# Decoder trunk step on eight cores: residual rows added by accumulating DMA, the mixing bias spread by matmuls, and three pieces of work moved

## The chip, the cores and the metric

The kernel runs on the 8 cores of one Trainium2 chip. Each core does one prompt sequence of 2048 positions and 64 sample rows (16 running sequences of 4 new tokens). No core talks to another. The metric is the device time in microseconds (us) of the slowest core.

## The reference

With x the residual rows, c the conditioning vector and D = 1024:

```python
mod = silu(c) @ w_ada + b_ada
shift, scale, gate = split(mod, 3)
h = rms_norm(x, g_norm) * (1 + scale) + shift
p = h @ w_in                                   # 3584 wide
h_a, b_a, c_a, z_a, u_b, v_b, z_b = split(p)
# group A: gated causal convolution of width 3
y_a = b_a * conv(c_a * h_a) * silu(z_a)
# group B: chunks of 128 positions, 8 heads
v_n = layer_norm(v_b)
y_b = u_b * (tril(w_s) @ v_n + b_s) * silu(z_b)
y = x + gate * (concat(y_a, y_b) @ w_out)
out = rms_norm(y, g_final)
```

Also returned are the last two rows of the convolution's input and the normalised v of the sample rows.

## The kernel before

Rows are worked in tiles of 128 positions and tiles in five blocks: 4, 4, 3 and the 64 sample rows, 3, and 2 tiles (`BLOCKS`, numbered 0 to 4). Channels lie on the partitions and positions along the free axis, so a projection is 8 matmuls of 128x128 weights against `hT` (up to 512 columns) into one PSUM bank. There are 8 banks, taken in turn by `nbank`, so a matmul group can start only when the engine that reads the group eight before it is done.

A block goes through two parts. In the **first part**, for j = 0 to 3, `A1` projects h and c (ACT copies the first out of its bank at L515, DVE multiplies at L523, ACT and DVE do the convolution at L534 and L541), and `A2` projects b and z (DVE L555, ACT L559, POOL L560 writes `yT`). After the pair of j = 2 (j = 1 in block 4) `V_group` projects v with the rows on the partitions (L601), DVE takes statistics (L616), and ACT writes the scaled `vn_bf` at L631. In the **gating part**, for j = 0 to 3, `GB` projects u and z (ACT L653, DVE L656), mixes `vn_bf` with `Wt` (PE L665), DVE adds the bias `bias2` (L675), and POOL multiplies into `yT` (L685). Between the steps of this part stands the **output step of the block before it**, one tile for each j: `C_mm` (PE L713, 16 matmuls of 512 columns), `C_s1` (DVE L729 and L730: times the gate, out of two banks; DVE L732: plus the residual rows, loaded again into `xc` by SP), `C_sq` (ACT L742: square sum), `C_s2` (DVE L800 and POOL L802: the power -1/2) and `C_s3` (DVE L811: times the norm factor, then a store by SP). `C_sq` of a tile is put off: `flush` issues it in the next `GB`, behind that `GB`'s first ACT instruction, and for the last tile of a block behind the gating part, which is ahead of the next block's first ACT copy (L515).

The input of the next block is made meanwhile: load into `xa`, square sum on ACT (`prep_sq`, L378), power on POOL (L380, L382), scaling on DVE (`prep_xn`, L389), transposes into `hT` (by PE for blocks 0 and 1, by DMA, L400, later), and `prep3`, the modulation with the adaLN scale and shift (ACT L428, DVE L432, for the sample columns DVE L443 and L446, which write all four k of a half).

Nothing reorders the work: every engine runs its instructions in the order in which the builder wrote them (`Sched`), and waits by semaphore at each. DMAs of the SP queue are issued by SP, the weights' and the first tiles' loads by POOL, in the same order of each queue's program. The bias `b_s` is brought to `bsT` by two SP loads that repeat one row over 64 partitions each (`late_loads_1`), and `bias2_ops` makes `bias2` of it.

Of the kernel before, what the change touches and what calls it, by code (L numbers as in the profile page):

```python
# [190 lines left out]
def build_nc(limit=None):  # L191
# [499 lines left out]
    def C_load(B, i, spare=None):  # L691
        ti, P, kind = B.tiles[i]
        R = slice(64, 128) if kind == "s" else slice(0, 128)
        src = x_s[0:64, :] if kind == "s" else x_p[(B.t0 + ti) * 128:(B.t0 + ti + 1) * 128, :]
        if spare is None:
            rc = nxt("xc", NXC)
            xt, xr = xc[rc], ("xc", rc)
        else:
            xt, xr = xa[spare], ("xa", spare)
        load("sp", xt[R, :], src, xr)  # L700
        cst[(B.i, i)] = [(xt, xr)]
# [474 lines left out]
```

How the kernel before makes its waits and increments, by code:

```python
        def run(e, eng):  # L113
            seen = {}
            nw = 0
            for o in streams[e]:
                need = {}
                waits = list(o.deps)
                if o.is_dma and o.prev is not None:
                    waits.append(o.prev)
                for d in waits:
                    key = d.sem.num
                    if key not in need or need[key][1] < d.val:
                        need[key] = (d.sem, d.val)
                for key, (sem, val) in need.items():
                    if seen.get(key, 0) >= val:
                        continue
                    eng.wait_ge(sem, val)
                    seen[key] = val
                    nw += 1
                ins = o.fn(eng)
                if o.is_dma:
                    ins.then_inc(o.sem, 16)
                elif o.needed:
                    ins.then_inc(o.sem, 1)
            stats[e] = (len(streams[e]), nw)
# [18 lines left out]
            @block.sync  # L155
            def _(eng):
                run("sp", eng)
                for q in self.QUEUES:
                    last = {}
                    for o in streams[q]:
                        if o.is_dma:
                            last[o.sem.num] = (o.sem, o.val)
                    for sem, val in last.values():
                        eng.wait_ge(sem, val)
```

## Time and profile before

| | us |
|---|---|
| median of 3 runs | 339.34 (338.82 to 340.24) |
| the profiled execution | 339.12 |
| its span, slowest core (4) | 337.3 |
| spans of the eight cores | 334.1 to 337.3 |
| busy: PE, DVE, ACT, POOL | 284.2, 187.7, 114.1, 110.7 |
| granted PE clock, mean | 0.968 |

1.8 us of the profiled execution lie outside the span. Times "at" a place count from the start of the span. On core 4, PE starts dense work at 48.9 us (block 0's second half of k), is in block 1 from 99.4 us, block 2 from 167.7, block 3 from 228.4, block 4 from 280.2, and ends its last matmul at 324.9. A busy PE means that matmuls are in flight, and idle time of PE before 325 us is what the path pays, as far as PE sets the end.

### The profile page before, as it was taken

How to read it: one execution, taken by the hardware profiler on the slowest of the kernel's cores; microseconds unless marked ns; L12 is line 12 of the kernel's file. 1: busy time of each engine (PE TensorE's matmuls, PEld its weight loads, DVE VectorE, ACT ScalarE, POOL GpSimd, SP SyncE). 2: the span in 40 equal slices, each digit the busy share in tenths (PEclk: the TensorE clock that was granted, in tenths of full speed). 3: DMA queues.
4: the chain of work that ended last, by engine and by line, in shares of the span. 5: the costliest groups of instructions: out<-in, count | busy, mean ns of one | idle time of the engine just before them, and what ended most of it. 6: DMA issues, size and time to landing. Idle time of an engine off the chain costs nothing.

```text
span 337.3 us, 5476 instructions; the slowest of 8 cores (334.1 to 337.3 us)
## 1 busy us (share of the span) xinstructions
PE 284.2 (84%) x1696; PEld 147.6 (44%) x1720; DVE 187.7 (56%) x350; ACT 114.1 (34%) x206; POOL 110.7 (33%) x161
## 2 busy tenths in 40 slices
PE   0325539999899999998989999999999999999840
PEld 0222214444454444443445454445555557766420
DVE  0321015445564454277887857658864666668982
ACT  2611013206552234311824245543216242232320
POOL 7294055214523531141224435121432112223210
PEclk9999858999999999999999999999999999999995
DMA  6999999999999992339327444212670102426223
GB/s 136 209 174 168 156 162 155 169 173 256 206 234 223 173 141 57 103 82 247 127 103 211 110 172 149 64 54 76 121 249 3 31 2 106 143 69 208 86 108 126
DMA packets 23148, 46.72 MB, mean 139 GB/s; under 512 B 10960, under 2 KB 11344, under 8 KB 22096
## 3 DMA queue, kind: packets, MB, share of 16 engines
q0 software_dynamic: 6624, 21.24, 35.0%
q1 hardware_dynamic: 16496, 25.14, 25.4%
q8 instruction: 14, 0.23, 0.3%
q14 instruction: 14, 0.11, 0.1%
HBM read 51.02 MB, written 8.85 MB: 178 GB/s over the span
## 4 chain that ended last, share of the span: by engine, by line
PE 42%; DMA 29%; DVE 12%; issue 7%; ACT 3%; POOL 3%; SPq 1%; DVEq 1%; POOLq 0%; ACTq 0%
PE pb L486 26%; DMA win_bf<-win_l 12%; DMA wada<-wada_l 11%; PE pb L713 8%; PE pb L601 4%; DVE ob L811 3%; DMA xa<-x_p 2%; DMA xc<-x_p 2%; DVE tmp L541 2%; DVE st L616 1%; PE pb L823 1%; ACT tmp L534 1%; POOL xa L314 1%; DVE ob L729 1%; DVE ob L730 1%
## 5 line engine op out<-in xcount | busy, mean ns | idle before, releaser
L486 PE MATMUL pb<-hT,win_bf 128*128 128x512 bf16 (+3 forms) x672 | 125.1, 341 | 2.0 <-DMA win_bf<-win_l 1.4
L486 PEld LDWEIGHTS pb<-hT,win_bf 128*128 128x128 bf16 x680 | 66.0, 98 | 57.5 <-issue 2.7
L713 PE MATMUL pb<-wout_bf,yT 128*128 128x512 bf16 (+1 forms) x246 | 56.6, 379 | 3.4 <-POOL yT L685 1.2
L486 PE MATMUL pb<-hT,wh 128*128 128x512 bf16 (+3 forms) x277 | 54.0, 356 | 4.7 <-ACT hT L428 3.6
L560 POOL TENSOR_TENSOR yT<-tmp,tmp 128x512 bf16<-128x512 f32 (+3 forms) x20 | 23.3, 1164 | 61.0 <-DVE tmp L555 32.3
L486 PEld LDWEIGHTS pb<-hT,wh 128*128 128x128 bf16 x280 | 27.8, 100 | 29.7 <-issue 9.8
L685 POOL TENSOR_TENSOR yT<-tmp,tmp 128x512 bf16<-128x512 f32 (+3 forms) x20 | 22.0, 1098 | 51.5 <-DVE tmp L675 27.6
L541 DVE SCALAR_TENSOR_TENSOR tmp<-spad,pv,tmp 128x512 f32<-128x512 f32 (+2 forms) x40 | 26.2, 656 | 20.7 <-ACT tmp L534 13.5
L713 PEld LDWEIGHTS pb<-wout_bf,yT 128*128 128x128 bf16 (+1 forms) x256 | 23.9, 98 | 29.9 <-issue 2.9
L601 PE MATMUL pb<-wv_bf,hT 128*128 128x512 bf16 (+1 forms) x133 | 29.6, 379 | 0.2
L742 ACT ACTIVATE junk<-ob 128x1024 bf16<-128x1024 f32 (+1 forms) x16 | 16.9, 1053 | 38.0 <-DVE ob L732 37.9
L389 DVE TENSOR_SCALAR xn<-xa,stat 128x1024 bf16<-128x1024 f32 (+1 forms) x17 | 13.7, 806 | 27.4 <-POOL stat L382 27.4
L428 ACT ACTIVATE hT<-hT,shT,aT 128x384 bf16<-128x384 bf16 (+2 forms) x28 | 18.0, 695 | 29.4 <-DVE aT L477 25.2
L534 ACT ACTIVATE tmp<-spad,pv 128x512 f32<-128x512 f32 (+2 forms) x20 | 12.7, 636 | 42.5 <-DVE spad L523 32.0
L523 DVE TENSOR_TENSOR spad<-pb,tmp 128x512 f32<-128x512 f32 (+2 forms) x20 | 11.7, 584 | 23.5 <-PE pb L486 11.6
L653 ACT ACTIVATE tmp<-pb 128x512 f32<-128x512 f32 (+3 forms) x20 | 10.3, 514 | 37.2 <-PE pb L486 37.2
L802 POOL TENSOR_TENSOR stat<-stat,mhalf 128x1 f32<-128x1 f32 x16 | 9.5, 596 | 37.2 <-DVE stat L800 24.5
L378 ACT ACTIVATE junk<-xa 128x1024 bf16<-128x1024 f32 (+1 forms) x17 | 17.9, 1054 | 11.1 <-DMA xa<-x_p 10.7
L732 DVE TENSOR_TENSOR ob<-ob,xc 128x1024 f32<-128x1024 f32 (+1 forms) x15 | 18.4, 1225 | 5.6 <-DMA xc<-x_p 3.3
L811 DVE SCALAR_TENSOR_TENSOR ob<-ob,stat,gf_bc 128x1024 f32<-128x1024 f32 (+1 forms) x16 | 20.5, 1279 | 1.5 <-POOL stat L802 1.4
L601 PEld LDWEIGHTS pb<-wv_bf,hT 128*128 128x128 bf16 (+1 forms) x136 | 13.3, 99 | 15.8 <-issue 0.4
L412 PE MATMUL pb<-ident,xn 128*128 128x128 bf16 x64 | 6.3, 263 | 16.0 <-DVE xn L389 16.0
(88 smaller groups left out, 252.9 us busy)
## 6 DMA issues: line engine op xcount, KB each, us to landing
y_p<-ob SPq DMA_DIRECT2D x15, 512.0 KB, 3.0
xc<-x_p SPq DMA_DIRECT2D x14, 512.0 KB, 6.9
wada<-wada_l POOLq DMA_DIRECT2D x6, 1024.0 KB, 35.4
xa<-x_p POOLq DMA_DIRECT2D x10, 512.0 KB, 39.1
win_bf<-win_l POOLq DMA_DIRECT2D x17, 256.0 KB, 42.7
xa<-x_p SPq DMA_DIRECT2D x8, 512.0 KB, 5.2
wout_bf<-wout_l POOLq DMA_DIRECT2D x2, 1024.0 KB, 57.7
wh<-winh_l POOLq DMA_DIRECT2D x4, 256.0 KB, 26.9
```

Of the source, the lines that this page charges most:

```text
L378: op("act", lambda e: e.activation(out=junk[0:P, :], in_=xa[ra][0:P, :], func=AF.Square, accum_out=ss), r=[("xa", ra)], w=[sres, "junk"])
L428: op("act", lambda e, k=k: e.activation(out=hb[:, k, 0:B.NP], in_=hb[:, k, 0:B.NP], func=AF.Identity, scale=aT[:, k, 0:1], bias=shT[:, k, ...
L486: ii = pe.matmul(bk.t[:, 0:B.N], lhsT=wsl(m, k), rhs=hT[B.h][:, k, 0:B.N], start=(k == 0), stop=(k == 7))
L534: ii = e.activation(out=c1[:, 0:NP], in_=spad[j][:, 2:2 + NP], func=AF.Copy, scale=cw(j, 2))
L541: ii = e.scalar_tensor_tensor(out=o[:, 0:NP], in0=spad[j][:, tp:tp + NP], scalar=cw(j, tp), in1=a[:, 0:NP], op0=ALU.mult, op1=ALU.add)
L560: op("pool", lambda e: e.tensor_tensor(out=yT[B.y][:, j, 0:N], in0=c2[:, 0:N], in1=sg[:, 0:N], op=ALU.mult), r=[c2r, sgr], w=[("yT", B.y, j)])
L601: ii = pe.matmul(bk.t[0:P, :], lhsT=hT[B.h][:, k, ti * 128:ti * 128 + P], rhs=wv_bf[:, k, :], start=(k == 0), stop=(k == 7))
L685: op("pool", lambda e: e.tensor_tensor(out=yT[B.y][:, 4 + j, 0:N], in0=tU[:, 0:N], in1=mb[:, 0:N], op=ALU.mult), r=[tUr, mbr], w=[("yT", B ...
L713: ii = pe.matmul(bk.t[R, :], lhsT=yT[B.y][:, k, ti * 128:ti * 128 + P], rhs=wout_bf[:, n, k, :], start=(k == 0), stop=(k == 7))
L732: op("dve", lambda e: e.tensor_tensor(out=o[R, :], in0=o[R, :], in1=xt[R, :], op=ALU.add), r=[ores, xr], w=[ores])
L742: op("act", lambda e: e.activation(out=junk[R, :], in_=o[R, :], func=AF.Square, accum_out=st[R, 0:1]), r=[ores], w=[sres, "junk"])
L811: op("dve", lambda e: e.scalar_tensor_tensor(out=o[R, :], in0=o[R, :], scalar=rs, in1=gf_bc[R, :], op0=ALU.mult, op1=ALU.mult), r=[ores, s ...
```

## The change

Five pieces. **One**: for the 15 output tiles of blocks 0 to 3, DVE's add of the residual rows (L732) and the SP loads into `xc` are gone. POOL issues, after DVE's two gate products, a DMA that reads the rows from `x_p` (or `x_s`) and adds them to `ob` in SBUF (`accum_op`). The square sum, the scaling and the store wait for this DMA. The two tiles of block 4 keep load and add. `ob` has 6 buffers for 3, in the room of `xc`. **Two**: the two repeating loads of `bsT` are replaced by a load of 2 rows, which DVE splits into three bf16 pieces (5 small instructions), and three matmuls with a 0/1 matrix (`sel`, three POOL instructions) that spread the sum of the pieces over the partitions; ACT copies the bank. This lies behind the first transposes. **Three**: in block 0, ACT scales v tiles 0 and 1 ahead of the convolution's first product of j = 3, and tiles 2 and 3 behind it, for all four behind it. **Four**: in block 1, `prep3` for block 2 moves from ahead of `GB` of j = 2 and 3 to behind `GB` of j = 1 and 2, ahead of the output step. **Five**: the multiply-add in `C_s2` (L800) moves from DVE to POOL, and in block 4 the final scaling of the last tile of block 3 moves from the step of j = 3 to behind `C_s1` of block 4's first tile.

```diff
-    NXC = 3
-    NOB = 3
+    NOB = 6
...
-    def A1(B, j):
+    def A1(B, j, mid=None):
...
+        if mid is not None:
+            mid()
         op("act", fc, r=sw + ["pv"], w=[c1r])
...
-        op("dve", lambda e: e.tensor_tensor(out=o[R, :], in0=o[R, :], in1=xt[R, :], op=ALU.add),
-           r=[ores, xr], w=[ores])
+        if own:
+            xt, xr = cst[(B.i, i)][0]
+            op("dve", lambda e: e.tensor_tensor(out=o[R, :], in0=o[R, :], in1=xt[R, :], op=ALU.add),
+               r=[ores, xr], w=[ores])
+        else:
+            src = x_s[0:64, :] if kind == "s" else x_p[(B.t0 + ti) * 128:(B.t0 + ti + 1) * 128, :]
+            op("pool", lambda e: e.dma_start(out=o[R, :], in_=src, accum_op=ALU.add), r=[ores], w=[ores], dma=True)
...
-        op("dve", lambda e: e.tensor_scalar(out=rs, in0=ss, scalar1=1.0 / D, scalar2=EPS, op0=ALU.mult, op1=ALU.add),
+        op("pool", lambda e: e.tensor_scalar(out=rs, in0=ss, scalar1=1.0 / D, scalar2=EPS, op0=ALU.mult, op1=ALU.add),
...
+    for q in range(3):
+        op("dve", lambda e, q=q: e.tensor_copy(out=bs_p[q], in_=bs_sb), r=["bias2"], w=[("vn", q)])
+        if q < 2:
+            op("dve", lambda e, q=q: e.tensor_tensor(out=bs_sb, in0=bs_sb, in1=bs_p[q], op=ALU.subtract),
+               r=["bias2", ("vn", q)], w=["bias2"])
+    bkb = nbank()
+
+    def fb(pe):
+        for q in range(3):
+            ii = pe.matmul(bkb.t[:, :], lhsT=sel, rhs=bs_p[q], start=(q == 0), stop=(q == 2))
+        return ii
...
-    def late_loads_1(g):
-        for half in range(2):
-            load("sp", bsT[64 * half:64 * half + 64, :, :].rearrange("p j t -> p (j t)"),
-                 bs_l[half].partition_broadcast(64), ("bsT", half), g)
...
-            A1(B, j)
+            A1(B, j, (lambda: V2(0, 2)) if b == 0 and j == 3 else None)
             if b == 0 and j == 3:
-                V2()
+                V2(2, 4)
...
-            if b == 1 and j >= 2:
-                prep3(NX, range(4 * j - 8, 4 * j - 4), "both")
...
+            if b == 1 and 1 <= j < 3:
+                prep3(NX, range(4 * j - 4, 4 * j), "both")
             if j < npv:
-                C_step(PV, j, (PV, j + NXC) if j + NXC < npv else None)
+                C_step(PV, j)
```

Where the instructions stand now. In the changed kernel the lines are numbered a few higher: L727 and L728 are the gate products (L729, L730 before), L736 the accumulating DMA, L745 the square sum (L742), L803 and L805 the norm factor (L800, L802), L429 and L433 to L447 the modulation (L428, L432 to L446), L661 and L680 the gating of `GB` (L656, L675), L516 the first copy of a block (L515).

On ACT, from the square sum of block 0's first output tile (`ob0`) to the first copy of block 2, before:

```order
L742 ACTIVATE junk_55,stat_82<-ob0_112 128x1024
L428 ACTIVATE hT0_47<-hT0_47,shT_76,aT_77 128x384 x2
L653 ACTIVATE tmp6_102<-pb4 128x512
L742 ACTIVATE junk_55,stat_82<-ob1_113 128x1024
L378 ACTIVATE junk_55,stat_82<-xa0_49 128x1024
L428 ACTIVATE hT0_47<-hT0_47,shT_76,aT_77 128x384 x2
L653 ACTIVATE tmp1_97<-pb1 128x512
L742 ACTIVATE junk_55,stat_82<-ob2_114 128x1024
L742 ACTIVATE junk_55,stat_82<-ob0_112 128x1024
L515 COPY tmp4_100<-pb5 128x448
```

and in the changed kernel:

```order
L745 ACTIVATE junk_55,stat_82<-ob0_109 128x1024
L429 ACTIVATE hT0_47<-hT0_47,shT_76,aT_77 128x384 x2
L658 ACTIVATE tmp6_102<-pb5 128x512
L745 ACTIVATE junk_55,stat_82<-ob1_110 128x1024
L429 ACTIVATE hT0_47<-hT0_47,shT_76,aT_77 128x384 x2
L379 ACTIVATE junk_55,stat_82<-xa0_49 128x1024
L658 ACTIVATE tmp1_97<-pb2 128x512
L745 ACTIVATE junk_55,stat_82<-ob2_111 128x1024
L745 ACTIVATE junk_55,stat_82<-ob3_112 128x1024
L516 COPY tmp4_100<-pb6 128x448
```

The second modulation stands ahead of the square sum of the next block but one's tile (`xa0`); each square sum of an `ob` now waits for a DMA.

On DVE, block 1's gating part, from the output product of tile 1 before:

```order
L729 TENSOR_TENSOR ob1_113<-pb1,gate_p_65 128x512
L730 TENSOR_TENSOR ob1_113<-pb2,gate_p_65 128x512
L732 TENSOR_TENSOR ob1_113<-ob1_113,xc1_110 128x1024
L800 TENSOR_SCALAR stat_82<-stat_82 128x1
L432 TENSOR_SCALAR hT0_47<-hT0_47,aT_77,shT_76 128x384 x2
L443 TENSOR_TENSOR tmp5_101<-hT0_47,aT_77 128x256
L446 TENSOR_TENSOR hT0_47<-tmp5_101,shT_76 128x4x64
L656 TENSOR_TENSOR tmp7_103<-pb3,tmp6_102 128x512
L675 SCALAR_TENSOR_TENSOR tmp8_104<-pb5,pv_78,bias2_68 128x512
L729 TENSOR_TENSOR ob2_114<-pb6,gate_p_65 128x512
L730 TENSOR_TENSOR ob2_114<-pb7,gate_p_65 128x512
```

and in the changed kernel, from `GB` of j = 1:

```order
L661 TENSOR_TENSOR tmp3_99<-pb7,tmp2_98 128x512
L680 SCALAR_TENSOR_TENSOR tmp4_100<-pb1,pv_78,bias2_68 128x512
L433 TENSOR_SCALAR hT0_47<-hT0_47,aT_77,shT_76 128x384 x2
L444 TENSOR_TENSOR tmp5_101<-hT0_47,aT_77 128x256
L447 TENSOR_TENSOR hT0_47<-tmp5_101,shT_76 128x4x64
L727 TENSOR_TENSOR ob1_110<-pb2,gate_p_65 128x512
L728 TENSOR_TENSOR ob1_110<-pb3,gate_p_65 128x512
L661 TENSOR_TENSOR tmp7_103<-pb4,tmp6_102 128x512
L680 SCALAR_TENSOR_TENSOR tmp8_104<-pb6,pv_78,bias2_68 128x512
L433 TENSOR_SCALAR hT0_47<-hT0_47,aT_77,shT_76 128x384 x2
L444 TENSOR_TENSOR tmp0_96<-hT0_47,aT_77 128x256
L447 TENSOR_TENSOR hT0_47<-tmp0_96,shT_76 128x4x64
```

The modulation of the first half (`hT0`) stands ahead of the product of tile 1, and that of the second half ahead of the product of tile 2 (which was ahead of it before); the add of 128x1024 is gone.

On POOL, block 4's gating part, from j = 0 before:

```order
L685 TENSOR_TENSOR yT0_95<-tmp6_102,tmp7_103 128x256
L685 TENSOR_TENSOR yT0_95<-tmp0_96,tmp1_97 128x256
L802 TENSOR_TENSOR stat_82<-stat_82,mhalf_83 128x1
L685 TENSOR_TENSOR yT0_95<-tmp3_99,tmp4_100 128x256
L802 TENSOR_TENSOR stat_82<-stat_82,mhalf_83 128x1
L685 TENSOR_TENSOR yT0_95<-tmp6_102,tmp7_103 128x256
L802 TENSOR_TENSOR stat_82<-stat_82,mhalf_83 128x1 x2
```

and in the changed kernel:

```order
L690 TENSOR_TENSOR yT0_95<-tmp6_102,tmp7_103 128x256
L736 DMA ob0_109<-x_p 128x1024
L690 TENSOR_TENSOR yT0_95<-tmp0_96,tmp1_97 128x256
L803 TENSOR_SCALAR stat_82<-stat_82 128x1
L805 TENSOR_TENSOR stat_82<-stat_82,mhalf_83 128x1
L736 DMA ob1_110<-x_p 128x1024
L690 TENSOR_TENSOR yT0_95<-tmp3_99,tmp4_100 128x256
L803 TENSOR_SCALAR stat_82<-stat_82 128x1
L805 TENSOR_TENSOR stat_82<-stat_82,mhalf_83 128x1
L736 DMA ob2_111<-x_p 128x1024
L690 TENSOR_TENSOR yT0_95<-tmp6_102,tmp7_103 128x256
```

Behind each `yT` product of j = 1 and 2 stands the norm factor of the tile before, and then the DMA of the tile of this step.

## Rows read from the trace of the kernel before

**Rows 1.** The page, busy time of each engine over the whole span.

```profile
PE 284.2 (84%) x1696; PEld 147.6 (44%) x1720; DVE 187.7 (56%) x350; ACT 114.1 (34%) x206; POOL 110.7 (33%) x161
```

**Rows 2.** The waits of PE: who waited for whom, us in total, times, longest.

```profile
PE pb L459 <- DMA wada<-wada_l: 14.0, 4, 4.9
...
PE pb L486 <- DMA win_bf<-win_l: 1.4, 1, 1.4
...
PE pb L486 <- DVE hT L446: 1.1, 1, 1.1
...
PE pb L713 <- DVE tmp L656: 0.9, 1, 0.9
```

**Rows 3.** The ten us from 80: busy by engine (count), clock, DMA share, GB/s.

```profile
80.00:90.00 10.00, 9.10 (x71) 4.50 (x69) 6.32 (x12) 6.44 (x12) 4.32 (x6) 1.00 1.05 224
```

**Rows 4.** Timeline of PE: start us, us, work, and idle before.

```profile
169.77 10.00 PE L486 MATMUL pb<-hT,wh 128*128 128x448 bf16 x52 [1.11 <-DVE hT L446]
...
194.29 9.26 PE L486 MATMUL pb<-hT,win_bf 128*128 128x448 bf16 x48
...
249.22 7.96 PE L486 MATMUL pb<-hT,win_bf 128*128 128x384 bf16 x48
...
320.86 0.59 PE L713 MATMUL pb<-wout_bf,yT 128*128 128x512 bf16 x2 [1.17 <-POOL yT L685]
```

**Rows 5.** The page, groups: the residual add on DVE, the power on POOL.

```profile
L732 DVE TENSOR_TENSOR ob<-ob,xc 128x1024 f32<-128x1024 f32 (+1 forms) x15 | 18.4, 1225 | 5.6 <-DMA xc<-x_p 3.3
...
L802 POOL TENSOR_TENSOR stat<-stat,mhalf 128x1 f32<-128x1 f32 x16 | 9.5, 596 | 37.2 <-DVE stat L800 24.5
```

**Rows 6.** The page, DMA issues: KB each, median us from issue to landing.

```profile
y_p<-ob SPq DMA_DIRECT2D x15, 512.0 KB, 3.0
...
xc<-x_p SPq DMA_DIRECT2D x14, 512.0 KB, 6.9
```

**Rows 7.** The DMA view, the 64 sample rows: KB, us to landing.

```profile
xc<-x_s SPq DMA_DIRECT2D x1, 256.0 KB, 3.5
```

**Rows 8.** The one load of `xa` issued at 177.8 us: its landing.

```profile
DMA to landing us min/median/max: 4.2/4.2/4.2
```

**Rows 9.** Timeline of DVE, gating part of block 1 and start of block 2.

```profile
152.28 0.68 DVE L730 TENSOR_TENSOR ob<-pb,gate_p 128x512 f32<-128x512 f32 x1
...
162.08 0.42 DVE L446 TENSOR_TENSOR hT<-tmp,shT 128x256 bf16<-128x256 f32 x1 [0.39 <-ACT hT L428]
...
169.54 0.75 DVE L389 TENSOR_SCALAR xn<-xa,stat 128x1024 bf16<-128x1024 f32 x1
...
172.06 0.68 DVE L730 TENSOR_TENSOR ob<-pb,gate_p 128x512 f32<-128x512 f32 x1
```

**Rows 10.** Timeline of ACT over the same stretch, and in block 2.

```profile
156.22 1.06 ACT L742 ACTIVATE junk<-ob 128x1024 bf16<-128x1024 f32 x1 [7.12 <-DVE ob L732]
...
160.67 1.31 ACT L428 ACTIVATE hT<-hT,shT,aT 128x384 bf16<-128x384 bf16 x2 [3.30 <-DMA hT<-xn]
...
175.34 0.51 ACT L515 COPY tmp<-pb 128x448 f32<-128x448 f32 x1
...
198.66 2.11 ACT L631 ACTIVATE vn_bf<-pb,stat 128x512 bf16<-128x512 f32 x3 [6.48 <-DVE stat L625]
```

**Rows 11.** Timeline of ACT in block 3 and at the start of block 4.

```profile
252.43 2.11 ACT L631 ACTIVATE vn_bf<-pb,stat 128x512 bf16<-128x512 f32 x3 [6.06 <-DVE spad L519]
...
284.81 0.37 ACT L515 COPY tmp<-pb 128x256 f32<-128x256 f32 x1
```

**Rows 12.** Timeline of DVE, last block.

```profile
281.41 0.69 DVE L730 TENSOR_TENSOR ob<-pb,gate_s 64x512 f32<-64x512 f32 x1
...
304.93 0.68 DVE L730 TENSOR_TENSOR ob<-pb,gate_p 128x512 f32<-128x512 f32 x1
...
325.05 0.68 DVE L768 TENSOR_TENSOR ob<-pb,gate_p 128x512 f32<-128x512 f32 x1
```

**Rows 13.** Timeline of POOL, last block.

```profile
319.99 0.72 POOL L685 TENSOR_TENSOR yT<-tmp,tmp 128x256 bf16<-128x256 f32 x1 [3.33 <-DVE stat L800]
```

More of the change, by code:

```diff
@@ L268, in build_nc @@
     vnS = A("vnS", [64, 512], F32)
+    sel = vn_bf[3][0:2, 0:128]
+    bs_sb = bias2[0:2, :, :].rearrange("p j t -> p (j t)")
+    bs_p = [vn_bf[q][0:2, :] for q in range(3)]
     yT0_off = (A.off + 63) // 64 * 64
@@ L276, in build_nc @@
     A.off = mark
-    NXC = 3
-    NOB = 3
-    xc = [A(f"xc{i}", [128, D], F32) for i in range(NXC)]
+    NOB = 6
     ob = [A(f"ob{i}", [128, D], F32) for i in range(NOB)]
@@ L585, in build_nc, with V2 @@
     vlate = []
-    def V2():
-        while vlate:
-            vlate.pop(0)()
+    def V2(q0=0, q1=4):
+        for f in vlate:
+            f(q0, q1)
+        if q1 == 4:
+            vlate.clear()
     def V_group(B, kind, grp, mid):
@@ L626, in V_group, with scale_v @@
                                                    op0=ALU.mult, op1=ALU.mult), r=[sres], w=[sres])
-        def scale_v():
-            for q, (ti, _) in enumerate(grp):
+        def scale_v(q0, q1):
+            for q, (ti, _) in list(enumerate(grp))[q0:q1]:
                 bk = bks[q]
@@ L689, in build_nc, with C_load @@
     cst = {}
[L691 to L701, printed above, removed]
+    def C_load(B, i):
+        load("sp", xa[i][:], x_p[(B.t0 + i) * 128:(B.t0 + i + 1) * 128, :], ("xa", i))
+        cst[(B.i, i)] = [(xa[i], ("xa", i))]
     def C_mm(B, i, k0, k1):
@@ L706, in C_mm @@
         if k0 == 0:
-            cst[(B.i, i)] += [nbank(), nbank()]
-        b0, b1 = cst[(B.i, i)][1:3]
+            cst[(B.i, i)] = cst.get((B.i, i), []) + [nbank(), nbank()]
+        b0, b1 = cst[(B.i, i)][-2:]
         def fn(pe):
@@ L720, in C_s1 @@
         R = slice(64, 128) if kind == "s" else slice(0, 128)
-        (xt, xr), b0, b1 = cst[(B.i, i)]
+        own = B.i == len(PB) - 1
+        b0, b1 = cst[(B.i, i)][-2:]
         g = gate_s if kind == "s" else gate_p
@@ L873, in build_nc @@
     cnt["xa"] = 0
+    load("sp", bs_sb, bs_l[:, :], "bias2")
     load("sp", st_sb[:].rearrange("p j s r -> p (j s r)"), stT[:, :], "st_sb")
@@ L881, in build_nc @@
        r=["ident"], w=["ident"])
+    op("pool", lambda e: e.memset(sel, 1.0), w=[("vn", 3)])
+    op("pool", lambda e: e.affine_select(out=sel, in_=sel, compare_op=ALU.is_ge, fill=0.0, base=0,
+                                         pattern=[[1, 128]], channel_multiplier=-64), r=[("vn", 3)], w=[("vn", 3)])
+    op("pool", lambda e: e.affine_select(out=sel, in_=sel, compare_op=ALU.is_ge, fill=0.0, base=63,
+                                         pattern=[[-1, 128]], channel_multiplier=64), r=[("vn", 3)], w=[("vn", 3)])
     for i, n in ((0, 2), (2, 2), (4, 3)):
@@ L891, in build_nc @@
     prep2(B0, 3, "act")
+    for q in range(3):
[8 more added lines that the diff above has]
+        return ii
+    op("pe", fb, r=[("vn", 3)] + [("vn", q) for q in range(3)], w=[bkb.res])
+    op("act", lambda e: e.copy(out=bsT[:].rearrange("p j t -> p (j t)"), in_=bkb.t[:, :]),
+       r=[bkb.res], w=[("bsT", 0), ("bsT", 1)])
     for i, n in ((0, 2), (2, 2), (4, 3)):
@@ L966, in C_step @@
         cq.append((B, i))
-        if nload is not None:
-            C_load(*nload)
         if len(cq) >= 3:
@@ L985, in build_nc @@
         late = b < 2
-        def first_c():
-            for i in range(min(NXC, npv)):
-                C_load(PV, i)
         if last:
             for i in range(len(B.tiles)):
-                C_load(B, i, i)
+                C_load(B, i)
         for j in range(4):
@@ L1108, in build_nc @@
             C_s1(B, 0)
+            C_s3(PV, npv - 1)
             C_mm_half(B, 1, 0)
```

11 lines of the change are left out of this document (2 added, 9 removed).

## The prediction

> **What bounds the kernel now.** I read four views in this order. The page gives PE 284.2 us of a span of 337.3 [rows 1], so PE carries the path but is idle for 53 us. The waits of PE say where: 14.0 us for the first weights, all before 48.9 us, and then little: 1.4 for a weight DMA late in block 0, 0.9 for DVE in block 1, 1.1 for the modulated input of block 2 [rows 2], 1.2 for the last `yT` [rows 4]. Behind PE's end at 324.9 us lie 12.4 us of closing work. So what can be won between 49 and 325 us is about 5 us, and much can be lost: PE runs dense only because the other engines hand back its 8 banks in time. The third view, the timelines of DVE and ACT, tells how much slack that has. The fourth, the DMA issues, tells how long a transfer takes to land.
>
> The DVE work taken away is large (the add takes 1.225 us [rows 5], 15 times), but its place is taken by a transfer on the same chain: gate product, residual, square sum on ACT. ACT is in order, so whatever stands behind the square sum waits for that DMA too. Call A the time from POOL's issue to the landing.
>
> **The price A.** No accumulating DMA is in the trace. Below stand the plain stores of the same 512 KB, 3.0 us, and above the loads into `xc`, 6.9 us in the median, which mostly ran three together [rows 6]. A single load of 512 KB from `x_p` took 4.2 us [rows 8]. The new DMA reads as much from `x_p` and also reads and rewrites `ob`, and POOL's issue is a little longer than SP's. The nearest row is the single load; I take A = 4.5, and keep 3.0 to 6.6. For the 64 sample rows the load took 3.5 [rows 7], 0.7 less than the full one, so A - 0.7 there.
>
> **Part by part.** A step from engine to engine is taken as 0.1 to 0.15 us: ACT ends its modulation at 160.67 + 1.31 = 161.98, DVE's L446 starts at 162.08 [rows 9, 10].
>
> *Startup.* Five small DVE instructions, three matmuls and three POOL instructions come at 5 to 24 us. PE waits there for weights anyway (14.0 us [rows 2]), and the first 48.9 us are bound by DMA: 0. If that cover were gone it would be about 1 us.
>
> *Bias load.* 256 KB of repeated rows leave the DMA engines in block 0, where these are saturated (share 1.05, 224 GB/s at 80 us [rows 3]): 256 KB at that rate is 1.2 us, by which the later weights land sooner. The wait there is 1.4: **-1.2**. The v tiles scaled sooner take some 0.6 us off PE's wait for banks before that, but the same weight DMA then sets the start: 0 (bounds of both together -2.0 and -0.5).
>
> *Block 1, gating.* The gate products of tile 0 end at 152.28 + 0.68 = 152.96 [rows 9], now 151.8. From there: steps, issue and landing 0.25 + A; square sum with its read 1.15; then ACT's half of the first modulation, 1.31 [rows 10], since it stands behind this square sum; DVE's L446, which waits for it (0.39 us already now [rows 9]), 0.5; only then the products of tile 1, 1.3. Then the same round again for tile 1 and the second half: 0.25 + A + 1.15 + 1.31 + 0.6. The input of block 2 is whole at 151.8 + 7.8 + 2A = 159.6 + 2A. Now it is at 169.77 [rows 4]; PE would be there at 168.66 - 0.87 - 1.2 = 166.6. With A = 4.5: 168.6. So **-1.2 against now** (this takes in the -1.2 above): the wait of 1.1 and that of 0.9 are not won but paid to the DMA. It is 2A - 10.2, never under -3.2.
>
> *Block 1 to 2.* Call E the time at which that input is whole. Behind E, DVE now has to do the products of tile 2 (1.3, before E until now), wait for POOL, which issues a DMA and runs two pairs for norm factors (a power 0.6 each [rows 5]) before the one that L389 needs (ends E + 4.7; it starts at 169.54 now [rows 9]), L656 and L675 (1.3), the products of tile 3 (1.3): E + 7.3, against 2.97 now (172.74 [rows 9]). Then DMA, square sum, and the first copy of block 2: it ends at E + 7.3 + 0.25 + A + 1.15 + 0.5 = E + 9.2 + A; now 175.34 + 0.51 [rows 10], E + 6.1. That is 3.1 + A later. What hangs on it is a chain of DVE and ACT, with no room in it, up to `vn_bf` in the same block: its first scaling ends at 199.4 [rows 10] and frees the bank in which PE puts u. PE's 48 matmuls from 194.29 are six groups of 1.54, u the fifth: it starts at 200.45 [rows 4]. Slack 1.05. So PE stands still for 3.1 + A - 1.05: **+6.5** with A = 4.5. Sum so far +5.3.
>
> *Block 2 to 3.* Here the order is the old one, and the add is replaced by the DMA: the first copy comes A - 1.7 later. The slack, read the same way, is 2.6 (the last of the three scalings from 252.43 [rows 11] against PE's mixing matmuls, after 249.22 and six groups [rows 4]): **+0.2**.
>
> *Block 3 to 4.* The products of the sample tile end at 282.1 [rows 12], the copy at 285.18 [rows 11]. They can start 0.4 sooner, since `ob` has six buffers. With A - 0.7 = 3.8 for the sample rows the copy comes 3.8 - 1.7 = **+2.1** later, and in block 4 (256 columns) the slack is only some 0.5, so DVE's chain and with it the end go by the whole.
>
> *Block 4 and the end.* Products of tile 0 end at 304.93 + 0.68 [rows 12] + D, where D is the shift so far. Its factor is ready A + 2.5 later; POOL issues the DMA of tile 1 behind it, so tile 1's factor comes at 310.6 + 2A + D; DVE's scaling of tile 1 (1.28) stands ahead of L656 and L675 (0.85) and POOL's last `yT` (0.8): 313.5 + 2A + D, which is 322.5 + D; now 319.99 + 0.72 = 320.7 [rows 13]: **+1.8**. Behind it DVE reaches L768 after 4.3 us now (325.05 [rows 12]); then it also waits for the factor of tile 2, A - 0.55 behind `yT`, and scales (1.28): A + 0.75 = 5.25: **+0.9**. The three adds gone here (3.7 us) are thus cover for waits, not a gain.
>
> Sum: -1.2 + 6.5 + 0.2 + 2.1 + 2.7 = +10.3. On the profiled execution's 339.1 that is **349.4 us**; the median of the runs is 339.34, 0.2 above it. All terms go by A: for A = 3.6 the sum is +4.2 (343.3), for A = 5.3 it is +16.7 (355.8), some 7 us for each us of A.
>
> **A rule against a row.** The row of plain stores says 3.0 us for 512 KB [rows 6], a load 4.2 [rows 8]. The Trainium skill (DMA: Bandwidth & Descriptors, Anatomy of one DMA, SWDGE path) gives for a DMA issued by GpSimd about 2.0 us plus the bytes over 436 GB/s, which is an estimate of 3.2 us here, and nothing extra for an accumulate; that would make the sum about +1.9, 341.0 us. No row shows this form of DMA.
>
> **The rivals.**
> (1) *The landing is as short as a store's.* A = 3.0: the input of block 2 is bound by PE (-3.2), 1.0 behind DVE's chain, so the stall in block 2 is 5.05 - 1.0; block 4's copy gives +1.3, the end -0.8. Sum +1.3: 340.4 us. For it: the stores. Against it: every load took longer.
> (2) *Faster.* The mechanism is that the square sums find their tile landed. It decides at A of about 2.8, by the sum above; with A = 2.0, as the 256 KB stores at the end take, the waits of 0.9 and 1.1 us and those of the end are won: -3.2, a stall of 4.05 - 3.0 in block 2, +0.3 into block 4, -1.7 at the end, sum -3.5: 335.6 us. For it: if my chain from the first copy of block 2 to `vn_bf` has more room than 1.0 us, the largest term falls away. Against it: the rows' 512 KB transfers.
> (3) *The landing is that of loads in company*, A over 5.3 up to 6.6, because the DMA moves each row twice or POOL writes its descriptors late. The sum is +17 to +27, middle 360 us. Against it: the DMA engines have room from 150 us on. The Trainium skill (SBUF — State Buffer, Who interferes with whom) says that DVE's two-port forms lock GpSimd out of the port with which it writes descriptors; that would lengthen A where L432 or L389 follows the product. No row here shows a DMA issue so held.
>
> **How the numbers follow.** My case (A 3.6 to 5.3) 0.58, rival 1 0.13, rival 2 0.16, rival 3 0.13. The range from 334.5 to 356.0 takes in all but rival 3 and a few strays. A measurement of this kernel tells about 0.5% from no change, 337.6 to 341.0: faster 0.16, same 0.13, slower 0.71.
>
> **What would show it.** In the changed profile: the accumulating DMA's landing, 4.5 us; ACT's square sum waiting for it, also ahead of the first copy of blocks 2, 3 and 4, with 6.4 us between the last gate product's end and that copy's end (3.1 now); PE idle some 6 us between 175 and 210 us, little at 260, some 2 us at 290 to 300; no wait for weights late in block 0; PE at block 2 near 168.6; POOL's last `yT` near 332. A landing under 3 us, or a dense PE in block 2, would refute the forecast.

## The result: 365.76 us, 7.6% slower

| | before | changed |
|---|---|---|
| median, us | 339.32 (338.82 to 340.24) | 365.76 (363.78 to 366.73) |
| ratio, 95% interval | | 1.0758 (1.0729 to 1.0788) |
| profiled execution; its span, slowest core | 339.12; 337.3 | 365.2; 363.6 |
| granted PE clock, that core | 0.968 | 0.949 |

The direction was forecast, the size was not: 349.4 us was said, with 356.0 as the upper end. Rival 3 (landings of 5.3 to 6.6 us, about 360 us) is the case that came, near its upper end. Medians below are over all executions of a kernel; the ratios leave out the few in which the cores of one die ran slower.

The page of the changed kernel, busy time of each engine and the DMA issues (KB, median us from issue to landing), to be read against [rows 1, 6]:

```profile
PE 298.1 (82%) x1723; PEld 149.3 (41%) x1723; DVE 171.8 (47%) x324; ACT 114.8 (32%) x207; POOL 129.8 (36%) x195
...
y_p<-ob SPq DMA_DIRECT2D x15, 512.0 KB, 4.8
ob<-x_p POOLq DMA_DIRECT2D x14, 512.0 KB, 6.2
```

DVE has 16 us less to do, as planned, and the span is 26.3 us longer. The median landing is 6.2 us, where the forecast took 4.5. PE's busy time grew too, by 13.9 us, and its idle time (span less busy) only from 53.1 to 65.5; what lies in the busy time is told in the last section.

The waits of ACT and of PE (us in total, times, longest), for [rows 2]:

```profile
ACT junk L745 <- DMA ob<-x_p: 86.3, 14, 12.2
...
PE pb L487 <- DVE ob L728: 4.5, 2, 4.2
PE pb L487 <- ACT tmp L516: 4.1, 2, 3.7
PE pb L710 <- POOL yT L690: 3.9, 1, 3.9
...
PE pb L487 <- DVE tmp L558: 2.4, 2, 1.8
PE pb L487 <- ACT vn_bf L636: 2.1, 2, 1.2
PE pb L487 <- DVE hT L447: 2.0, 1, 2.0
```

All 15 square sums of these tiles wait for their DMA: 14 in the row above, and that of the sample tile for 3.0 us. From block 1 on PE never waits for a DMA itself; it waits for DVE, ACT and POOL in turn, and the chain shows how these stand behind ACT. Here is the chain that ended last, over 150 to 200 us (start, us, what):

```profile
150.04 0.68 DVE ob L728
...
151.35 8.81 DMA ob<-x_p
...
161.45 1.21 ACT hT L429 x2
...
163.69 0.69 DVE ob L728
...
164.99 7.22 DMA ob<-x_p
...
174.00 0.70 ACT hT L429
...
182.14 1.10 POOL yT L690
...
183.73 7.30 DMA ob<-x_p
...
192.32 0.43 ACT tmp L516
```

Gate product, DMA, square sum, modulation, next gate product, DMA: this is the round that the forecast wrote down, twice in block 1 and once more into block 2, with 8.8, 7.2 and 7.3 us where it put 4.5. PE over the same stretch and at the end ([rows 4] before):

```profile
164.52 3.57 PE L487 MATMUL pb<-hT,win_bf 128*128 128x512 bf16 x8 [4.20 <-DVE ob L728]
...
175.37 0.92 PE L487 MATMUL pb<-hT,wh 128*128 128x448 bf16 x4 [2.04 <-DVE hT L447]
...
192.89 4.87 PE L487 MATMUL pb<-hT,win_bf 128*128 128x448 bf16 x16 [3.68 <-ACT tmp L516]
...
215.57 3.19 PE L487 MATMUL pb<-hT,win_bf 128*128 128x448 bf16 x16 [0.93 <-ACT vn_bf L636]
...
346.19 0.59 PE L710 MATMUL pb<-wout_bf,yT 128*128 128x512 bf16 x2 [3.90 <-POOL yT L690]
```

The input of block 2 is whole at 175.37 (169.77 before), block 3 starts at 243.65 (228.44), block 4 at 298.10 (280.20), and the last `yT` is done at 346.05 (320.7). These are the slowest cores of either profile, core 5 here and core 4 before.

### The profile page after: what moved, and what is told of

It reads as the page before. It is cut to its first block, busy times and chain, and to the rows that moved or that the text cites. A ratio compares the mean times of both kernels' runs of the same rounds, so it can differ in the third digit from the quotient of the medians.

```text
span 363.6 us, 5517 instructions; the slowest of 8 cores (357.6 to 363.6 us)
## 1 busy us (share of the span) xinstructions
PE 298.1 (82%) x1723; PEld 149.3 (41%) x1723; DVE 171.8 (47%) x324; ACT 114.8 (32%) x207; POOL 129.8 (36%) x195
## 4 chain that ended last, share of the span: by engine, by line
PE 34%; DMA 27%; DVE 13%; issue 12%; POOL 5%; ACT 4%; DVEq 1%; SPq 1%; POOLq 0%; ACTq 0%
PE pb L487 20%; DMA ob<-x_p 13%; DMA wada<-wada_l 10%; PE pb L710 8%; PE pb L606 5%; DVE tmp L544 2%; DVE st L621 2%; DMA xa<-x_s 2%; DMA ob<-x_s 1%; DVE spad L524 1%; DVE ob L728 1%; ACT tmp L535 1%; ACT junk L745 1%; DMA hT<-xn 1%; POOL yT L690 1%
## 5 line engine op out<-in xcount | busy, mean ns | idle before, releaser
L487 PE MATMUL pb<-hT,win_bf 128*128 128x512 bf16 (+3 forms) x680 | 130.6, 348 | 13.1 <-DVE ob L728 4.2
L487 PEld LDWEIGHTS pb<-hT,win_bf 128*128 128x128 bf16 x680 | 66.3, 99 | 73.2 <-issue 20.9
L710 PE MATMUL pb<-wout_bf,yT 128*128 128x512 bf16 (+1 forms) x256 | 58.5, 381 | 5.6 <-POOL yT L690 3.9
L487 PE MATMUL pb<-hT,wh 128*128 128x512 bf16 (+3 forms) x280 | 57.4, 367 | 5.4 <-DVE hT L433 2.9
L745 ACT ACTIVATE junk<-ob 128x1024 bf16<-128x1024 f32 (+1 forms) x16 | 16.9, 1058 | 89.5 <-DMA ob<-x_p 86.3
L487 PEld LDWEIGHTS pb<-hT,wh 128*128 128x128 bf16 x280 | 28.4, 103 | 33.2 <-issue 14.8
L544 DVE SCALAR_TENSOR_TENSOR tmp<-spad,pv,tmp 128x512 f32<-128x512 f32 (+2 forms) x40 | 27.0, 674 | 21.1 <-ACT tmp L535 14.7
L429 ACT ACTIVATE hT<-hT,shT,aT 128x384 bf16<-128x384 bf16 (+2 forms) x28 | 18.1, 698 | 21.8 <-DVE aT L478 20.5
L736 POOL DMA_DIRECT2D ob<-x_p x14 | 12.9, 922 | 31.6 <-DVE ob L728 15.8
L636 ACT ACTIVATE vn_bf<-pb,stat 128x512 bf16<-128x512 f32 x16 | 11.4, 778 | 27.2 <-DVE stat L630 16.4
L381 POOL TENSOR_SCALAR stat<-stat 128x1 f32<-128x1 f32 (+1 forms) x17 | 4.3, 250 | 38.9 <-ACT junk L379 38.0
```

What stands on the lines that cost most here:

```text
L429: op("act", lambda e, k=k: e.activation(out=hb[:, k, 0:B.NP], in_=hb[:, k, 0:B.NP], func=AF.Identity, scale=aT[:, k, 0:1], bias=shT[:, k, ...
L487: ii = pe.matmul(bk.t[:, 0:B.N], lhsT=wsl(m, k), rhs=hT[B.h][:, k, 0:B.N], start=(k == 0), stop=(k == 7))
L544: ii = e.scalar_tensor_tensor(out=o[:, 0:NP], in0=spad[j][:, tp:tp + NP], scalar=cw(j, tp), in1=a[:, 0:NP], op0=ALU.mult, op1=ALU.add)
L710: ii = pe.matmul(bk.t[R, :], lhsT=yT[B.y][:, k, ti * 128:ti * 128 + P], rhs=wout_bf[:, n, k, :], start=(k == 0), stop=(k == 7))
L745: op("act", lambda e: e.activation(out=junk[R, :], in_=o[R, :], func=AF.Square, accum_out=st[R, 0:1]), r=[ores], w=[sres, "junk"])
```

## Experiments

The kernels of one group ran on one chip, with runs of the kernel before beside them; ratios are to those. The edits are shown cut (`...`) and without the switches that select them in the kernels that ran.

### Is it the DMA, or the new order?

`e1_no_accum` undoes part one and keeps parts two to five.

```diff
-    NOB = 6
+    NXC = 3
+    NOB = 3
...
-            op("pool", lambda e: e.dma_start(out=o[R, :], in_=src, accum_op=ALU.add), r=[ores], w=[ores], dma=True)
+            op("dve", lambda e: e.tensor_tensor(out=o[R, :], in0=o[R, :], in1=xt[R, :], op=ALU.add),
+               r=[ores, xr], w=[ores])
```

> Part one of the change is undone: residual rows are loaded into `xc` by SP and added by DVE, with three buffers of each, as before; the parts two to five (bias by matmuls, v tiles, third block's modulation, norm factor on POOL) stay. My theory: all of the loss hangs on the accumulating DMA between gate product and square sum, and the other parts win the two small waits of block 1 and the weight wait. Then 336 to 340 us, input of block 2 whole at 168 to 169, block 2's stall gone. Rival: the new order by itself costs, since DVE's products of tiles 2 and 3 come behind the modulation and the norm factors move to POOL: then 345 us or more, with block 2's last gating groups still late on PE.

Measured 339.61 us beside 339.55, ratio 1.0006 (0.9983 to 1.0028). The rival falls: parts two to five cost nothing. Nor do they win anything that is measured. In the profiled execution, averaged over the eight cores, block 1's first matmul comes at 98.0 us for 99.2, as much as the forecast had for the bias load, and the mean span is 334.5 us for 335.6. Over all executions of this group (10 and 13) little of that is left: the mean span of the cores is 335.1 us for 335.4, which is within the scatter, and the slowest core, which is the metric, has 338.2 for 337.8.

`e2_accum_alone` is part one on the order of before; this edit undoes part four, and the others go back in the same way.

```diff
-            if b == 1 and 1 <= j < 3:
-                prep3(NX, range(4 * j - 4, 4 * j), "both")
...
+            if b == 1 and j >= 2:
+                prep3(NX, range(4 * j - 8, 4 * j - 4), "both")
```

> Part one alone: the accumulating DMA on the order of before, parts two to five undone (modulation of block 2 ahead of `GB` of j = 2 and 3, L800 on DVE). My theory: the loss is the landing on the square-sum chain in each block, so most of it stays. Block 2's input is whole near 170, but DVE's L800 now waits for ACT's square sum, which waits for the DMA: 350 to 362 us. Rival: the loss comes from what the other parts add to the DMA (the modulation chained behind two landings, POOL's longer queue): then 346 us or less.

Measured 367.38 us, ratio 1.0829 (1.0782 to 1.0877). All of the loss is in part one alone. My range ended at 362 us, since I had expected the old order to soften the loss, and it doesn't. Two of its waits say why: besides ACT (L770 is the square sum here), DVE now waits too, since the multiply-add of the norm factor (L800 before, L828 here) is still on DVE and holds it for the square sum.

```profile
ACT junk L770 <- DMA ob<-x_p: 79.4, 13, 11.1
...
DVE stat L828 <- ACT junk L770: 33.5, 11, 7.8
```

### What makes the landing long?

Three kernels keep the place of the DMA and change the DMA. `e3_plain_pool` and `e4_plain_sp` copy the rows without adding, so they leave out the gate product in the 15 tiles:

```diff
-            op("pool", lambda e: e.dma_start(out=o[R, :], in_=src, accum_op=ALU.add), r=[ores], w=[ores], dma=True)
+            op("pool", lambda e: e.dma_start(out=o[R, :], in_=src), r=[ores], w=[ores], dma=True)   # e3
+            op("sp", lambda e: e.dma_start(out=o[R, :], in_=src), r=[ores], w=[ores], dma=True)     # e4
```

> All of the change, but the DMA that POOL issues into `ob` is a plain copy of the same rows (no accumulate), in the same place of the same queue; it leaves out the gate product in those 15 output tiles. If the accumulate itself makes the landing long: median landing 4.2 to 4.7 us and, at some 7 us of time for each us of landing, 349 to 354 us. If POOL's issue and queue make it long, the landing stays near 6 and the time near 365 us.

> As the plain copy on POOL's queue, but issued by SP, still behind the gate product; the gate product is left out of those tiles again. If what POOL does costs (0.9 us of issue, and its queue), the landing falls to 4.2 as for the single load of before and the time to 345 to 350 us; if a 512 KB read from `x_p` has its time from the DMA engines alone, it is within 0.3 us of the POOL copy's landing and within 3 us of its time.

`e8_half` moves half of the bytes, with the accumulate, and leaves out the residual of the other half of the columns:

```diff
+            H = slice(0, 512)
-            op("pool", lambda e: e.dma_start(out=o[R, :], in_=src, accum_op=ALU.add), r=[ores], w=[ores], dma=True)
+            op("pool", lambda e: e.dma_start(out=o[R, H], in_=src[:, H], accum_op=ALU.add), r=[ores], w=[ores], dma=True)
```

> The changed kernel, but the accumulating DMA moves columns 0 to 511 only (256 KB for 512; the residual of the other columns is left out in the 15 output tiles). If the landing is bytes at a rate, its median falls from 6.2 to near 3.3 us; if most is a fixed part (as 4.4 to 4.7 for the 64 sample rows against 5.3 in the same blocks says), it is 5 to 5.5 us. At 7.5 us of time for each us of landing, 344 us or 357 to 360 us.

The DMA issues on the pages of e3, e4 and e8, in this order:

```profile
ob<-x_p POOLq DMA_DIRECT2D x14, 512.0 KB, 4.7
```

```profile
ob<-x_p SPq DMA_DIRECT2D x14, 512.0 KB, 3.5
```

```profile
ob<-x_p POOLq DMA_DIRECT2D x14, 256.0 KB, 4.4
```

| 15 transfers per core | landing, us | time, us |
|---|---|---|
| plain, issued by SP, 512 KB | 3.5 | 345.56 (two runs) |
| accumulating, POOL, 256 KB | 4.4 | 351.31 (one run, another chip) |
| plain, issued by POOL, 512 KB | 4.7 | 354.59 (two runs) |
| accumulating, POOL, 512 KB | 6.2 | 365.76 |

Neither expectation for e3 and e4 was all of it: 1.2 us of the landing come with POOL in place of SP, 1.5 more with the accumulate. In these four kernels the time follows the landing, whatever makes it: (365.76 - 345.56) / (6.2 - 3.5) = 7.5 us for each us, and the two in the middle lie within 1.1 us of that line (7.6 with each time taken as its difference to the kernel before on the same chip: +26.4 and +6.0). My expectation for e8 was wrong on both sides: half of the bytes saves 1.8 us of landing. From the two sizes an accumulating landing is 2.6 us and another 3.6 us for each 512 KB; that is a line through two points, and the one sample tile does not follow it: 4.4 us with 256 KB in the changed kernel, 4.6 with 128 KB here.

### Is it the landing, or what stands behind it?

`e5_hold` has the same DMAs and moves the square sums, factors and scalings one step later.

```diff
     def flush(keep=1):
-        while sqp:
-            C_sq(*sqp.pop(0))
+        while len(sqp) > keep:
+            sq1()
...
+            if j == 0:
+                flush(0)
+                if not last:
+                    s3n()
+                s2n()
```

(`sq1` issues the square sum of the oldest tile, `s2n` its factor, `s3n` its scaling.)

> The whole change, accumulating DMA included, but each square sum stands one gating step later on ACT (behind the first ACT instruction of the `GB` after next, the last tile's behind the next block's first copy), and norm factor and final scaling one step later too. No work is left out or added. My theory: the DMA costs only because the square sum that waits for it stands ahead of ACT's work for the path; with a landing of 5.5 to 7 us and steps of 7 us it has landed when ACT gets there. ACT's 86 us of waits for `ob` nearly vanish, PE's stalls in block 2 go, and the adds taken off DVE are won at last: 334 to 340 us. Rival: the DMA costs by itself (POOL's issue of 0.9 us, its queue held by a wait for DVE's products, traffic in SBUF): 350 us or more, although ACT does not wait.

Measured 338.32 us beside 337.36, ratio 1.0021 (1.0003 to 1.0040). All but 1 us of the 26 is gone, and all 15 accumulating DMAs are still there, with a median landing of 6.2 us. So the landing costs by its place ahead of ACT's other work. What POOL's issue and the traffic cost beside it is 1 us, less whatever the adds taken off DVE win in this order. One part of the expectation was wrong: ACT's waits for the DMA didn't nearly vanish. Of ACT's and of PE's waits in this kernel:

```profile
ACT junk L773 <- DMA ob<-x_p: 32.3, 9, 6.0
```

```profile
PE pb L506 <- ACT vn_bf L655: 0.7, 1, 0.7
```

32.3 us are left, and hardly any of it reaches PE: its longest wait from block 1 on is the second row, 0.7 us. In this kernel block 2 starts at 165.63, block 3 at 225.06 and block 4 at 276.82, 2.1 to 3.4 us ahead of the kernel before; 1.6 us of that are there at block 1's start already (97.80 for 99.37). This lead is what I had called the gain, and none of it reaches the end. I come back to it below.

### Which block pays?

`e6_acc_first` and `e7_acc_last` keep the accumulating DMA for one block's tiles, with load and add for the rest (three buffers each of `xc` and `ob`).

```diff
-        own = B.i == len(PB) - 1
+        own = B.i != 0          # e6: only block 0's tiles accumulate
+        own = B.i != 3          # e7: only block 3's
```

> The change, but the accumulating DMA for the four tiles of block 0 alone (issued in block 1's gating part); the tiles of blocks 1 to 3 have load and add again, with three buffers each. In the changed kernel block 3 started 15.2 us later than before, 1.2 us won on the weights included. My theory, each block pays for its own landings: 339.6 + 15 = 353 to 357 us. By the terms of my forecast at the landings of 6.4 to 8.8 us seen here: -1.2 becomes about +4, +6.5 becomes +9, so 352 to 353. Rival: a block's delay is absorbed by slack later or grows with those of others: under 349 or over 359.

> The change, but the accumulating DMA for the three tiles of block 3 alone (issued in block 4's gating part). My theory: in the changed kernel the span grew by 8.4 us after block 4's start, of which the sample tile's landing before it takes some 3; then 344 to 346 us here. If POOL's queue in block 4 alone makes the whole of it, 348 us; if it was only the tail of earlier delay or the lower clock that follows earlier stalls, 341 us or less.

Measured beside 337.36: e6 352.99 (ratio 1.0464, 1.0430 to 1.0498), that is +15.6; e7 343.45 (1.0167, 1.0138 to 1.0195), +6.1. Both lie at or just under the lower end of my ranges, since the kernel before took 337.4 on this chip, not 339.6; as differences they are what the trace of the changed kernel gave: +15.2 up to block 3's start, and 8.4 from block 4's start less 2.7 for the sample tile. With the 2.7 us that the trace has for each of the two blocks not run alone the sum is 27.1 us, for 26.4 of the whole: the losses add up block by block, to within a microsecond.

### Where does the lead go, and can the change win?

`e9_hold_ladd` keeps the held order for blocks 0 to 2 and gives block 3's tiles a load (straight into their output buffer) and an add.

```diff
+        ladd = B.i == len(PB) - 2
-        op("dve", fn, r=[b0.res, b1.res] + gr, w=[ores])
+        op("dve", fn, r=[b0.res, b1.res] + gr, w=["scr" if ladd else ores])
+        if ladd:
+            op("dve", lambda e: e.tensor_tensor(out=o[R, :], in0=o[R, :], in1=scr[R, :], op=ALU.add), r=[ores, "scr"], w=[ores])
```

> The held order (square sums one step later, accumulating DMA) for the twelve tiles of blocks 0 to 2; the three tiles of block 3 are loaded straight into their output buffer by SP one block ahead, DVE writes the gate products into a scratch tile and adds, and block 4 has the changed kernel's own order (square sum, factor and scaling one step behind). No work is left out. With the held order block 4 began 3.4 us sooner than before (276.8 against 280.2), but the end of the last matmul won nothing and the scalings of three tiles crowded behind it. My theory: block 4 and the closing work took 56.5 us in the kernel without accumulate, so 276.8 + 56.5 = 333.4 us of span and 335 to 336 us, 1 to 1.3% under before. Rival: the closing work is bound by DVE's total work from block 4 on, and three more adds give it all back: 338 us or more.

Measured 337.81 us beside 337.77, ratio 1.0015 (0.9992 to 1.0038): the expected 1% did not come. The profiled core starts block 4 at 275.94, but at its end PE waits for `yT`, `yT` for DVE, and DVE, busy for 9.6 of 10 us from 300 us on, has the scaling of the tile before ahead of it. The timelines of PE, DVE and POOL:

```profile
319.07 0.59 PE L747 MATMUL pb<-wout_bf,yT 128*128 128x512 bf16 x2 [1.71 <-POOL yT L713]
```

```profile
316.04 1.29 DVE L858 SCALAR_TENSOR_TENSOR ob<-ob,stat,gf_bc 128x1024 f32<-128x1024 f32 x1 [0.58 <-POOL stat L849]
317.24 0.42 DVE L684 TENSOR_TENSOR tmp<-pb,tmp 128x256 f32<-128x256 f32 x1
```

```profile
314.24 1.64 POOL L849 TENSOR_TENSOR stat<-stat,mhalf 128x1 f32<-128x1 f32 x1
```

`e10_late_scale` moves that scaling behind the two DVE instructions that `yT` needs:

```diff
             if last:
                 GB(B, j, (lambda j=j: C_sq(PV, j - 1)) if 0 < j <= npv else None)
+                if j > 1:
+                    C_s3(PV, j - 2)
                 if j > 0:
                     C_s2(PV, j - 1)
...
-                elif j < npv:
-                    C_s3(PV, j - 1)
```

`e11_late_no_accum` makes the same edit in the kernel of e1, without any accumulating DMA.

> The held order with loads and adds for block 3's tiles, and one thing more: in block 4 the final scaling (1.28 us on DVE) of tiles 0 and 1 of block 3 moves behind the next `GB`'s two DVE instructions. In the kernel before this one DVE did 9.6 of 10 us from 300 us on, the last `yT` came at 318.2 us, and PE waited 0.5 and 1.7 us there, while block 4 had begun 4.3 us sooner than in the kernel before the change. My theory: DVE's order in block 4 gives the lead back; the last `yT` then comes at some 317 us, the closing work starts 1.5 us sooner, and the time is 336.3 us, 0.4% under before. Rival: the closing work behind the last `yT` is bound by DVE's sum of work whatever its order, 337.8 us again.

> The kernel without accumulating DMA (loads into `xc`, adds by DVE, parts two to five of the change) with the same later scaling in block 4, as the control for the run above. It has not the 4 us lead of the held order at block 4's start (280.75 there against 275.9). If the accumulate's gain counts for anything, this is 1 us or more slower than its partner, 338 to 339.5 us; if only the order in block 4 counts, both are alike at 336 to 337 us.

Measured beside 337.60: e10 336.33 us, ratio 0.9965 (0.9947 to 0.9983); e11 337.44, ratio 1.0003 (0.9982 to 1.0024). e10 is faster than the kernel before by 0.35%, which is 1.2 us. That is less than I had said a measurement here can tell, but its interval excludes 1. The control, which has neither the DMA nor the held order, shows no gain. PE at the end of e10:

```profile
318.63 0.59 PE L748 MATMUL pb<-wout_bf,yT 128*128 128x512 bf16 x2 [0.48 <-POOL yT L714]
319.06 3.62 PE L800 MATMUL pb<-wout_bf,yT 128*128 128x512 bf16 x16
```

The last wait is 0.5 us for 1.7. Since e10's profiled core began block 4 at 277.44, 1.5 us later than e9's, and still reached this point 0.4 us sooner, block 4 itself is 1.9 us shorter. Behind it come 16 us of closing work in e10, e9 and the kernel before alike (334.9 - 319.06; 337.3 less 321.3). So twelve adds taken off DVE, 12 x 1.225 = 14.7 us, together with the held order, are worth 1.2 us (1.1 against e11); how much of that is the order's own was not run.

## Why the forecast missed, step by step

The working was built on A. Put the landings that the trace of the slowest core shows into its own formulas (the trace column is that core against the slowest of before):

| step of the forecast | said | by its formula, measured landings | trace |
|---|---|---|---|
| input of block 2, against 169.77 | -1.2 | 159.6 + 8.8 + 7.2 - 169.8 = +5.8 | +5.6 |
| block 1 to 2 (PE's stall) | +6.5 | 2.05 + 7.3 = +9.4 | +9.6 |
| block 2 to 3 | +0.2 | 7.1 - 4.3 = +2.8 | +2.7 |
| block 3 to 4 and last `yT` | +3.9 | (4.4 - 1.7) + (5.6 + 5.3 - 7.2) = +6.4 | +7.4 |
| closing work | +0.9 | 5.3 + 0.75 - 4.3 = +1.8 | +1.0 |
| sum | +10.3 | +26.2 | +26.3 |

That the sum closes to 0.1 us is in part luck. The gate products of tile 0 ended 1.1 us sooner than written down (150.72 for 151.8), and the round behind them took 0.9 longer. On core 4, which was the slowest before, the span grew by 21.4 us, and the formulas with its own landings (7.8 and 6.0, then 6.3, 6.7, 4.6, 5.8, 5.5 and 5.5) give 23.3. The mean span of the eight cores grew by 24.8, the delay at block 3's start is 10.1 to 17.2 us from core to core. So the formulas are good to some 2 us, not to 0.1.

**The mechanism was right**: the chain through the square sum, ACT's order, which block pays, and that the adds gone are no gain. The slope was said as some 7 us for each us (8 by its own terms once A is over 4.3) and measured as 7.5. e1 and e5 show where the loss sits, e6 and e7 which blocks pay. One sign of the forecast was too simple: it had PE stand still for all of the stall in block 2. Of the 9.6 us there, PE is idle for 5.7 (0.3, 0.3, 3.7, 0.5 and 0.9); the rest is matmuls that took longer, up to the last wait at 215.57.

**The step that failed is the price A.** I took 4.5 us from the single load [rows 8], as the nearest row, and so counted the second pass over the tile and POOL's issue as 0.3 us. The POOL issue alone brought the plain copy to 4.7, and the accumulate brought it to 6.2. It was also not one number: the two landings on the most expensive place, in block 1, took 8.8 and 7.2 us, those of whole tiles in block 4 5.3 to 5.6. With the median of 6.2 the formulas give +24.0. Both rivals with a short A had a slip too: their term for the copy of block 4 is A - 1.7, without the 0.7 for the sample rows, so their sums should be 0.7 lower. It changed nothing.

**The range failed with it.** 3.0 to 6.6 was written down for A, and rival 3 had the sum for its upper end, +27; yet the case with A over 5.3 got a chance of 0.13 and the range was cut below it. The row for loads in company, 6.9 us [rows 6], was dismissed since the DMA engines have room from 150 us on. In part they hadn't (the last three numbers are the granted clock, the DMA share and GB/s):

```profile
150.00:160.00 10.00, 10.00 (x54) 4.47 (x52) 4.11 (x7) 0.00 (x0) 2.30 (x2) 1.00 0.80 170
...
183.00:192.00 9.00, 6.21 (x33) 3.02 (x31) 1.63 (x3) 1.98 (x3) 2.06 (x4) 1.00 0.82 151
```

These two stretches are those of the landings of 8.8 and 7.3 us. But over the landing of 7.2 us, 165.0 to 172.2, the share was 0.45:

```profile
165.00:172.20 7.20, 7.20 (x32) 2.76 (x31) 1.54 (x4) 0.00 (x0) 3.30 (x4) 0.70 0.45 76
```

So room on the engines is no proof of a short landing either.

**The weights.** "No wait for weights late in block 0" was right on the profiled core; four of the eight cores still waited there, 0.5 to 1.9 us (seven before, 0.2 to 2.3). Averaged over the cores block 1 started 0.8 us sooner (98.4 for 99.2). e1 shows that this was not worth its 1.2 us on the slowest core.

**The rule against the row.** The Trainium skill's formula (DMA: Bandwidth & Descriptors, Anatomy of one DMA, SWDGE path) gave an estimate of 3.2 us. The runs measured 4.7 for the plain copy on POOL's queue and 6.2 with the accumulate. The measurement decides: rival 1, which rested on such a landing, is refuted. The Trainium skill's other rule, on DVE holding GpSimd off (SBUF — State Buffer, Who interferes with whom), showed little in the issue: POOL's instruction took 888 to 1015 ns in all 15 cases. The two longest, 998 and 1015, are the two with DVE's modulation (L433) beside them, at most 0.1 us more than the others. Behind the issue DVE can't have held up much of the longest landing, that of 8.8 us from 151.35 on: over its last six us DVE was busy for 0.11 us, ACT and POOL not at all, and the DMA engines nearly the whole time.

```profile
154.00:160.00 6.00, 6.00 (x36) 2.62 (x33) 0.11 (x1) 0.00 (x0) 0.00 (x0) 1.00 0.91 221
```

That landing is the first of block 1, and it is a long one on cores 0, 4 and 7 as well (8.0, 7.8 and 8.5 us). The company of other transfers is the likely reason, but no run took it away, so it stays open, as does the reason for the 7.2 us.

## What to carry to other kernels

Price a transfer that goes onto a chain by what happens if it lands like the slowest row of its size, and ask first which in-order engine waits for it and what stands behind that wait: here each microsecond of landing cost 7.5, and all 15 transfers together cost 1 us once the waiting instructions stood one step later. Work taken off an engine that does not set the pace is worth only what its order lets through (14.7 us of adds and a changed order, 1.2 us of time). Where the price of a new operation is not in the trace and the sum goes 7 to 1 by it, the range must go to the price's own end.

## What the hardware showed that was not expected

- An accumulating DMA of 512 KB lands 6.2 us after its issue in the median (4.4 for 256 KB), a plain one from POOL 4.7, and one from SP 3.5, in the same place of the same kernel. POOL's issue instruction takes 0.92 us with the accumulate and 0.63 without.
- The stores of 512 KB landed later in the changed kernel too, 4.8 us in the median for 3.0 [rows 6]; with the same DMAs in the held order of e5 they took 3.4. I have no cause for it.
- The granted clock falls after the stalls. Two stretches of ten us, busy by engine (count), clock, DMA share, GB/s:

```profile
160.00:170.00 10.00, 5.80 (x23) 2.01 (x22) 3.79 (x8) 2.83 (x5) 3.32 (x4) 0.66 0.32 53
170.00:180.00 10.00, 7.68 (x31) 3.20 (x30) 2.84 (x5) 3.87 (x7) 2.39 (x5) 0.83 0.16 27
```

  Before, both were at 1.00. So PE ran for part of them at 1.2 GHz in place of 2.4, after waits of 4.2 and 2.0 us: the 8 matmuls of 512 columns behind the first wait took 3.57 us, 8 of them otherwise 1.89. Over the whole span the matmuls of L487 took 348 and 367 ns in the mean for 341 and 356 (L486), which on 960 of them is some 8 us; of PE's 13.9 us of more busy time the rest is in part matmuls missing from the earlier record. In block 2 PE still waited 0.93 us behind the slow matmuls, for ACT, so there they were hidden behind the chain; that the lower clock cost nothing anywhere is not shown. At the end, the 16 matmuls of 512 columns behind the last `yT` took 5.30 us for 3.62 before, and the closing work as a whole was 1.0 us longer.
- A POOL instruction is stretched by DVE. The power on 128x1 took 1.63 and 1.64 us in e9 where it began together with DVE's 128x1024 add, and 0.55 behind the last `yT`. In e10 two `yT` products took 1.64 and 1.63 us in place of 0.72, each beside DVE's scaling. The Trainium skill (SBUF — State Buffer, Who interferes with whom) says that a DVE instruction with two SBUF inputs and a GpSimd instruction that reads SBUF shut each other out, the second waiting for the first to end. The trace agrees: the scaling beside the second product ended at 317.90 (316.62 + 1.28), the product 0.58 us behind it.

```profile
316.62 1.28 DVE L859 SCALAR_TENSOR_TENSOR ob<-ob,stat,gf_bc 128x1024 f32<-128x1024 f32 x1
```

```profile
316.85 1.63 POOL L714 TENSOR_TENSOR yT<-tmp,tmp 128x256 bf16<-128x256 f32 x1 [1.84 <-DVE tmp L704]
```
